# First layer's shift as two extra columns of keys, values and queries, and its scale weights loaded first

## The reference

```python
sh1, sc1, gt1, sh2, sc2, gt2 = modulation(cond, w_mod, b_mod)   # silu(cond) @ w_mod + b_mod
h = rms_norm(x, norm1_g) * (1.0 + sc1) + sh1
q, k, v, u = mixer_projections(h, w_in, ...)     # one product; q and k then normed per head
attn = block_attention(q, keys, vals)            # 8 heads, 2 key heads, head width 64
pooled = pool_mixer(u, w_pool, pool_scale)       # windowed mean minus self, 4 windows
x = x + gt1 * (concat(attn, pooled) @ w_out)
h2 = rms_norm(x, norm2_g) * (1.0 + sc2) + sh2
x = x + gt2 * conv_ffn(h2, w_up, conv_w, conv_b, w_down)
```

## Time and profile before

| | us |
|---|---|
| median of 3 runs (lowest, highest) | 1436.96 (1436.85, 1437.48) |
| the profiled execution | 1439.71 |
| its span, first to last instruction | 1437.9 |
| granted TensorE clock, mean | 0.996 |
| PE busy | 1405.4 (98%) |
| VectorE busy | 907.0 (63%) |
| ScalarE busy | 534.4 (37%) |
| GpSimd busy | 398.6 (28%) |

### The profile page before, as it was taken

One profiled execution on the slowest core, in us unless ns is written; L12 is line 12 of the kernel. 1 busy time (PEld: TensorE's weight loads), 2 busy tenths in 40 slices (PEclk: granted clock), 3 DMA queues, 4 the chain that ended last, 5 costly groups with the idle time before them and its releaser, 6 DMA issues.

```text
span 1437.9 us, 24974 instructions
## 1 busy us (share of the span) xinstructions
PE 1405.4 (98%) x9867; PEld 1347.5 (94%) x9867; DVE 907.0 (63%) x1429; ACT 534.4 (37%) x798; POOL 398.6 (28%) x273
## 2 busy tenths in 40 slices
PE   6999999999999999999999999999999999999998
PEld 3888889999999999999999877999999999999998
DVE  3548879897966478785775887369844323444333
ACT  5427863533231123332242687244232112332332
POOL 0165002053430033434214800213433101323321
PEclk9999999999999999999999999999999999999999
DMA  9752014253535334344413200224323312222321
GB/s 317 226 183 96 2 31 133 90 152 110 163 122 164 94 115 143 124 120 150 125 56 89 62 2 2 59 89 132 103 74 88 90 57 74 73 73 73 101 61 74
DMA packets 198158, 147.03 MB, mean 102 GB/s; under 512 B 4401, under 2 KB 187449, under 8 KB 197049
## 3 DMA queue, kind: packets, MB, share of 16 engines
q1 hardware_dynamic: 196592, 144.27, 32.8%
q10 hardware_dynamic: 1480, 1.57, 0.3%
HBM read 142.94 MB, written 2.88 MB: 101 GB/s over the span
## 4 chain that ended last, share of the span: by engine, by line
PE 83%; DVE 9%; ACT 2%; issue 2%; SPq 1%; DMA 1%; DVEq 0%; ACTq 0%
PE pair L1506 65%; PE pair L1522 7%; PE pair L1916 3%; PE pair L1961 3%; PE pair L1930 2%; DVE mod_acc L1073 2%; DVE conv L1423 1%; DVE in_lo L1139 1%; DVE w_lo L1050 1%; DVE norm_t L1129 1%; SPq L427 1%; DMA w_first<-in_w_mod_dram 1%; DVE small L1352 1%; PE pair L1759 1%; PE pair L1662 0%
## 5 line engine op out<-in xcount | busy, mean ns | idle before, releaser
L1506 PE MATMUL pair<-in_hi,w_hi 128*128 128x384 f32 x1728 | 395.7, 310 | 2.8 <-DVE w_lo L1050 2.8
L1506 PE MATMUL pair<-in_lo,w_hi 128*128 128x384 f32 x1728 | 394.6, 309 | 0.0
L1506 PE MATMUL pair<-in_hi,w_lo 128*128 128x384 f32 x1728 | 393.0, 308 | 0.0
L1423 DVE SCALAR_TENSOR_TENSOR conv<-pair,vec,conv 128x127 f32<-128x127 f32 x352 | 168.6, 542 | 192.8 <-ACT conv L956 192.4
L1506 PEld LDWEIGHTS pair<-in_hi,w_hi 128*128 128x128 f32 x1728 | 264.8, 188 | 8.3 <-DVE w_lo L1050 3.7
L1506 PEld LDWEIGHTS pair<-in_lo,w_hi 128*128 128x128 f32 x1728 | 265.3, 189 | 0.0
L1506 PEld LDWEIGHTS pair<-in_hi,w_lo 128*128 128x128 f32 x1728 | 264.0, 188 | 0.0
L653 POOL TENSOR_TENSOR silu_a<-silu_a,conv 128x640 f32<-128x640 f32 x44 | 108.6, 2469 | 538.7 <-DVE conv L1423 538.7
L956 ACT ACTIVATE conv<-pair,vec 128x640 f32<-128x640 f32 x88 | 77.8, 886 | 409.7 <-PE pair L1506 407.4
L1050 DVE TENSOR_TENSOR w_lo<-w_raw,w_hi 128x1024 fp32r<-128x1024 f32 (+1 forms) x148 | 195.6, 1322 | 38.3 <-ACT w_hi L675 38.0
L675 ACT ACTIVATE w_hi<-w_raw 128x1024 fp32r<-128x1024 f32 (+1 forms) x82 | 97.0, 1183 | 289.7 <-PE pair L1506 272.9
(11 more groups left out here) (210 smaller groups left out, 1773.1 us busy)
## 6 DMA issues: line engine op xcount, KB each, us to landing
w_raw<-in_w_up_dram SPq DMA_DIRECT2D x88, 512.0 KB, 3.8
mod_raw<-in_w_mod_dram SPq DMA_DIRECT2D x64, 512.0 KB, 4.2
w_raw<-in_w_down_dram SPq DMA_DIRECT2D x32, 704.0 KB, 4.6
w_raw<-in_w_in_dram SPq DMA_DIRECT2D x20, 512.0 KB, 4.1
w_first<-in_w_mod_dram SPq DMA_DIRECT2D x16, 512.0 KB, 9.3
w_raw<-in_w_out_dram SPq DMA_DIRECT2D x16, 512.0 KB, 4.0
mod_raw<-in_w_mod_dram SPq DMA_DIRECT2D x4, 1024.0 KB, 5.0
mod_acc<-in_w_mod_dram SPq DMA_DIRECT2D x4, 1024.0 KB, 5.0
```

The source lines that it names most:

```text
L1423: ins = dve.scalar_tensor_tensor(out=conv[:, s, d0:d1], in0=up_result(g, j, s)[:, d0 + sh:d1 + sh], scalar=v(L, V_TAP[t], s * NF + g * FG ...
L1506: ins = pe.matmul(dst[:, a:e], w[:, s, k, :], rhs[:, kk, a:e], start=first and r == 0, stop=last and r == 2)
```

## The change

The normalised features of layer 0 no longer contain the shift: `in_hi` and `in_lo` hold x times norm times gain, made in one operation for each segment. The shift itself becomes two columns (one for each conditioning) behind the 640 of each feature, split into high and low like the rest. Keys, values and queries of layer 0 are multiplied with 642 columns, and the product of the two last columns is added as a bias when ScalarE takes the tile out of PSUM, segment by segment. The pooled part u needs no shift, since a constant falls out of a mean minus self.

The modulation weights are loaded in eight parts of 1 MB: f = 0 to 3 scale, f = 4 to 7 shift. Only the scale parts stand before the first products. The sums of parts 4 and 5 stand ahead of tile 2, their turning behind it, those of parts 6 and 7 and `mod_second(0)` inside tile 3. Parts 6 and 7 are loaded into the place of the scaled x, after the last low part has been made. The rows of vectors are turned in two steps instead of one, the table for the root is loaded ahead of the squares, x tile 7 is copied by ScalarE instead of VectorE, and rows of the first modulation lie in `v_feat` instead of `mod_acc`. The diff, cut to its core:

```diff
+        XE_SCALAR, XE_VECTOR = [4, 6, 7], [0, 1, 2, 3, 5]
 
 
         with ExitStack() as inputs:
-            in_hi = sb("in_hi", [P, NK, T], F32R, at=inputs)
-            in_lo = sb("in_lo", [P, NK, T], F32R, at=inputs)
+            TX = T + 2
+            in_hi_x = sb("in_hi", [P, NK, TX], F32R, at=inputs)
+            in_lo_x = sb("in_lo", [P, NK, TX], F32R, at=inputs)
...
             def load_first(f):
 
-                if f >= N_FIRST:
-                    sp.wait_ge(s_mfirst, f - N_FIRST + 1)
-                for h in range(2):
-                    for ch in range(2):
-                        src = w_mod[0][h * D // 2:(h + 1) * D // 2, ch * D + f * 2 * P:ch * D + (f + 1) * 2 * P]
-                        sp.dma_start(w_first[:, f % N_FIRST, ch, h * NK // 2:(h + 1) * NK // 2, :],
-                                     src.rearrange("(i p) n -> p i n", p=P)).then_inc(s_first[2 * f + h], 16)
+                if f == 4:
+                    sp.wait_ge(s_mfirst, 1)
+                elif f == 5:
+                    sp.wait_ge(s_mfirst, 3)
+                elif f == 6:
+                    sp.wait_ge(s_h, 2 * NK)
+                ch, at = (1, f) if f < NK // 2 else (0, f - NK // 2)
+                src = w_mod[0][:, ch * D + at * 2 * P:ch * D + (at + 1) * 2 * P]
+                sp.dma_start(first_place[f], src.rearrange("(i p) n -> p i n", p=P)).then_inc(s_first[f], 16)
...
                 load_first(f)
-            for n in range(2, 4):
-                load_in(0, n)
+            load_in(0, 2)
+            load_first(4)
+            load_first(5)
+            load_in(0, 3)
+            load_first(6)
+            load_first(7)
             sp.dma_start(cst[:, P:n_const - P], consts[:, P:n_const - P]).then_inc(s_const, 16)
             load_second(0)
...
+            first_row(0)
+            x_copy(XE_SCALAR[0])
+            columns(0)
             hi(0, 0, NK)
-
-
+            x_copy(XE_SCALAR[1])
+            x_copy(XE_SCALAR[2])
+            hi(1, 1, NK)
...
-                        act_e.wait_ge(s_vec_t, L + 2)
-                        for t in range(3):
-                            ins = act_e.activation(vec[:, L, t, 0:N_ROWS[t]], pair[L][:, t * P:t * P + N_ROWS[t]], ACT.Copy)
-                        ins.then_inc(s_vec, 1)
-                    hi(1, 1, NK)
                 act_e.wait_ge(*((s_fmod, k + 1) if k < NK - 1 else (s_gain, 1)))
-                act_e.wait_ge(s_xhat, k + 1)
-                if k >= 2:
-                    act_e.wait_ge(s_h, 2 * (k - 1))
+                act_e.wait_ge(s_nt, 2 * (k + 1))
                 for ci, a, b in SEG:
-                    act_e.activation(sq[:, k % 2, a:b], xhat[:, k, a:b], ACT.Identity,
-                                     scale=gain[:, 0, 0, ci, k:k + 1],
-                                     bias=mod[:, 0, 0, ci, k:k + 1]).then_inc(s_nt, 1)
-                act_e.wait_ge(s_nt, 2 * (k + 1))
-                act_e.activation(in_hi[:, k, :], sq[:, k % 2, :], ACT.Copy).then_inc(s_hhi, 2)
+                    act_e.activation(in_hi[:, k, a:b], xhat[:, k, a:b], ACT.Copy,
+                                     scale=gain[:, 0, 0, ci, k:k + 1]).then_inc(s_hhi, 1)
+                if k in (2, 4):
+                    first_row(k // 2 + 1)
+                if k == 6:
+                    columns(1)
...
                     e = e_of(n)
+                    shifted = L == 0 and n >= IN_K
+                    if shifted:
+                        columns_ = pair[n % 2][:, LIN0 + T:LIN0 + TX]
+                        act_e.activation(shift_out[:, n - IN_K, 0, :], columns_, ACT.Copy).then_inc(s_shift_out, 1)
+                        if n >= IN_Q:
+                            act_e.activation(shift_out[:, n - IN_K, 1, :], columns_, ACT.Copy,
+                                             scale=v(L, V_QG, 0)).then_inc(s_shift_out, 1)
+                        act_e.wait_ge(s_shift_out, n - IN_K + 1 + max(0, n - IN_Q + 1))
+
+                    def evict(dst, func, own=0):
+                        for ci, a, b in SEG:
+                            ins = act_e.activation(dst[:, a:b], lin[n % 2][:, a:b], func,
+                                                   bias=shift_out[:, n - IN_K, own, ci:ci + 1],
+                                                   scale=v(L, V_QG, 0) if own else 1.0)
+                        return ins
...
-            for k in range(2):
-                scaled_x(k)
-            lo(0, 0, NK)
+                for t in range(2):
+                    if f < NK // 2:
+                        m = 2 * f + t
+                        dve.tensor_scalar(gain[:, 0, 0, :, m], first_sum[:, f % 2, t, :], v(0, V_N1, m),
+                                          first_gain[:, m:m + 1], ALU.mult, ALU.add)\
+                           .then_inc(*((s_fmod, 1) if m < NK - 1 else (s_gain, 1)))
+                    else:
+                        m = 2 * f + t - NK
+                        ins = dve.tensor_scalar(mod[:, 0, 0, :, m], first_sum[:, f % 2, t, :], v(0, V_BMOD, m), None, ALU.add)
+                        if m == NK - 1:
+                            ins.then_inc(s_mod, 2)
...
+                dve.wait_ge(s_shift_hi, 1)
+                dve.tensor_tensor(in_lo_x[:, :, T:TX], mod[:, 0, 0, :, :].rearrange("p c k -> p k c"),
+                                  in_hi_x[:, :, T:TX].bitcast(F32), ALU.subtract).then_inc(s_shift, 1)
+
             dve.wait_ge(s_vec, 1)
             dve.scalar_tensor_tensor(out=first_gain[:, :], in0=v(0, V_BMOD, NK, NK), scalar=1.0, in1=v(0, V_N1, 0, NK),
                                      op0=ALU.add, op1=ALU.mult).then_inc(s_fgain, 1)
             dve.wait_ge(s_fgain, 1)
             first_mod(0)
+            dve.wait_ge(s_bc, 1)
+            scaled_x(0)
             lo(1, 1, NK)
+            scaled_x(1)
             for k in range(NK):
+                for ci, a, b in SEG:
+                    dve.wait_ge(s_hhi, 2 * k + 1 + ci)
+                    dve.scalar_tensor_tensor(out=in_lo[:, k, a:b], in0=xhat[:, k, a:b], scalar=gain[:, 0, 0, ci, k:k + 1],
+                                             in1=in_hi[:, k, a:b].bitcast(F32), op0=ALU.mult,
+                                             op1=ALU.subtract).then_inc(s_h, 1)
+                if k % 2 == 0 and k // 2 + 1 < NK // 2:
+                    first_mod(k // 2 + 1)
                 if k + 2 < NK:
                     scaled_x(k + 2)
-                if k % 2 == 1 and k + 1 < NK:
-                    first_mod((k + 1) // 2)
-                dve.wait_ge(s_hhi, 2 * (k + 1))
...
+                    if L == 0 and n == 2:
+                        first_mod(4)
+                        first_mod(5)
                     if n >= IN_Q:
                         shuffle(e_of(n))
                     if n == N_IN - 1:
@@ -1331,6 +1402,10 @@
                         shuffle(0)
                     if 2 <= n < 2 + NPOOL:
                         window_end(n - 2)
+                    if L == 0 and n == 2:
+                        first_mod(6)
+                        first_mod(7)
+                        shift_low()
...
+            def first_sums(f):
+                pe.wait_ge(s_first[f], 16)
+                if f == 1:
+                    pe.wait_ge(s_vec, 1)
+                elif f == 4:
+                    pe.wait_ge(s_nt, 2 * NK)
+                elif f == 6:
+                    pe.wait_ge(s_u, 6)
+                if f >= 2:
                     pe.wait_ge(s_fsum, f - 1)
-                for i in range(4):
-                    ins = pe.matmul(first_bank(f)[i * QUAD:(i + 1) * QUAD, :].rearrange("p (c n) -> p c n", c=2),
-                                    cond_cols[:, 4 * h + i, :], w_first[:, f % N_FIRST, :, 4 * h + i, :],
-                                    start=h == 0, stop=h == 1)
-                if h == 1:
-                    ins.then_inc(s_mfirst, 1)
+                for k in range(NK):
...
+                if k == 3:
+                    first_sums(0)
+                if k == 4:
+                    rows_turned(0)
+                if k == 5:
+                    first_columns(0)
             pe.wait_ge(s_rstd, 1)
             spread_tiles(range(NT)).then_inc(s_bc, 1)
-            for h in range(2):
-                first_sums(0, h)
-            N_ROW_DMAS = 5 + 4 + 3 + DEPTH
-            pe.wait_ge(s_rows, 16 * N_ROW_DMAS)
-            for L in range(DEPTH):
-                x_emptied(NK - 2 + L)
-                for t in range(3):
-                    ins = pe.transpose(pair[L][:, t * P:t * P + N_ROWS[t]], rows[0:N_ROWS[t], L, t, :],
...
-
-                    def first_ahead(k):
-                        f = k // 2 + 1 if k % 2 == 0 else k // 2 + 2
-                        if k == 0:
-                            first_sums(1, 0)
-                        if f < NK // 2:
-                            first_sums(f, 1 if k % 2 == 0 else 0)
+                    x_emptied(NK - 2)
+                    x_emptied(NK - 1)
+                    keep_busy(3, pair[0][:, 0:P])
 
```

(63 more changed lines are left out.)

108 lines of the change are left out of this document (57 added, 51 removed).

## The result

| | us |
|---|---|
| kernel before, median of 5 runs | 1437.29 |
| changed kernel, median of 5 runs (lowest, highest) | 1443.70 (1443.4, 1444.8) |
| ratio, 95% interval | 1.0047 (1.0033 to 1.0062) |
| profiled execution of the changed kernel | 1444.8, span 1443.0 |
| forecast | 1434.8 (1431.0 to 1439.0) |

What follows compares the result with a forecast made beforehand. PE was taken as the bound, with the start bound by bytes in the SP queue. Front gain 5.0 - 1.9 - 0.9 - 0.1 = 2.1, say 2.2 us, off the median 1436.96 gives 1434.8, range 1431.0 to 1439.0.

Steps and rivals of the forecast that it cites:

- Point 9: Behind the first scores: later stages are untouched and PE-bound, so what is gained at the first scores stays gained.
- Point 8: Tiles 4 to 9: the two extra columns cost 0.1 us in the sum, bounds 0 and 2.2.
- Points 1 to 3: Front: f1 lands at 21.9, first product at 24.4 (gain 7.0), third tile ends at 52.5 (gain 8.9).
- rival B: New front: the clock falls again (2.5 us) or f1 is late (1.5), giving 1436.5 to 1437.5; chance 0.20.
- point 2: From f1 to first product: PE starts at 24.4 against 31.46; table load hidden, even at the quoted 2.66 us.
- Point 5: Tile 3, SP's new wait: w_in 4 lands at 60.3, s_shift at 65.4, tile 4 starts at 65.5; front gains 5.0.
- rival C: Queue behind SP's new wait: w_in 4 after 60.5 loses time one for one; 1441.0 at 250 GB/s; chance 0.08.
- Point 6: Evictions of tiles 4 to 9: ScalarE needs 1.0 to 1.1 more a query tile; PE waits 1.9 in tile 9.
- Point 7: Tile 9 to first scores: serial ScalarE adds 1.05, VectorE wins part back; 0.9 lost, bounds 0.3 and 1.1.

Runs made afterwards that it cites:

- b_pitch642: Kernel before with only the rows of in_hi and in_lo widened to 642 floats (2568 bytes), cond_rows moved to make room: 1441.74 us, ratio 1.0033.
- a_turn672: a_pitch672 plus constants and mod_second 0 and 1 issued ahead of f6 and f7, and ScalarE's copy second_rows ahead of k_out: 1431.03 us, ratio 0.9954.
- a_pitch656: Changed kernel with rows of in_hi and in_lo of 656 floats (2624 bytes) in place of 642: 1444.01 us.
- a_pitch672: Changed kernel with rows of in_hi and in_lo of 672 floats (2688 bytes), shift_out and first_gain moved to make room: 1436.38 us, ratio 0.9993.
- a_plain_evict: Changed kernel with the evictions of the kernel before for tiles 4 to 9 (no shift_out, no bias, one segment each): 1439.98 us.
- a_loads: Changed kernel with the constants and mod_second 0 and 1 issued ahead of loads f6 and f7: 1440.30 us, ratio 1.0023 of before.
- b_base64: Kernel before with an unused 64-byte array ahead of in_hi, moving array starts, pitch still 2560 bytes: 1435.48 us, ratio 0.9991.
- b_base32: Kernel before with an unused 32-byte array ahead of in_hi, starts at multiples of 128 bytes, pitch 2560: 1427.08 us, ratio 0.9950, in two groups.
- b_mix: Kernel before with only in_lo moved, to 32 bytes beyond a multiple of 64, in_hi at a multiple of 64, pitch 2560: 1443.09 us, ratio 1.0037.
- b_off48: Kernel before with in_hi and in_lo both starting 48 bytes beyond a multiple of 64, pitch 2560: 1447.12 us, ratio 1.0068.

## Why the prediction was wrong

The waits of the front and of tile 9 were read rightly. The time was lost by the price of a matmul, which the sum put at almost nothing, by a baseline that the median run doesn't have, and by VectorE's small and late instructions beside GpSimd.

- **Point 9, later stages untouched, failed.** "What is gained at the first scores stays gained" is true for waiting, not for the price of a matmul. The changed kernel loses 3.3 us behind the first scores. *b_pitch642*, where nothing but the rows changed, loses 5.5 there and 4.8 in its median.
- **Point 8 named the cause and mis-sized it.** It says that no row shows a row of `in_hi` that starts 8 bytes off, and bounds the cost at 2.2, for the six tiles with the extra columns. But the pitch belongs to the array, and every product that reads it in both layers pays: 5184 matmuls, not 144. It measured 4.3 behind the first scores, where I had taken 0.1. The extra columns themselves were sized well: with the pitch mended a tile with them takes 7.26, and one of the same shape without them (at 203.15 in *a_turn672*) 7.22, 0.2 us in all.
- **The sum's own baseline failed.** The gain was read off an execution with half clock from 29 to 35, 2.75 us over the median, and taken from the median in full. I had written how the two stand to each other, and then carried 5.0 over as if the median run had that stretch too. With tile 4 at 67.6 in executions without it, the gain at 65.5 would have been 2.1, and the forecast 2.1 - 1.9 - 0.9 - 0.1 = -0.8, that is 1437.8: no gain at all, or next to none if the median run has a short fall. What the front gave is less still: tile 4 starts at 67.25 to 67.64 in the four profiles with this front (the changed kernel, *a_pitch656*, *a_pitch672*, *a_plain_evict*), 0.5 ahead of 67.8 at most.
- **Points 1 to 3 held**: f1 22.2 (21.9), first product 24.67 (24.4), third tile's end 52.1 (52.5), no half clock there (rival B). The table load took 1.28 (9.08 to 10.36) and the next activation began at 10.38, less than the figure that point 2 quotes.
- **Point 5 held up to VectorE.** w_in 4 was in at 60.8 (60.3); the columns of f6 became possible at 62.21 (62.2), and PE waited 0.9 for them. Then two `first_mod` took 2.0 more than sized, beside two instructions of GpSimd: `s_shift` at 67.4, not 65.4. I had taken their price from rows without GpSimd at work. The fall of the clock in tile 4 (1.6) comes and goes with the execution: of the four profiles with this front and this wait, the changed kernel and *a_pitch672* have it, *a_pitch656* and *a_plain_evict* don't. *a_loads*, without the wait, is 3.0 to 3.4 faster in the median. That is rival C's mechanism, the queue behind SP's new wait, at much less than its price, and coming on top rather than in place.
- **Point 6 held**: PE's wait in the middle of tile 9 is 1.66 (1.9), and it goes with the additions (*a_plain_evict*) or with an earlier copy (*a_turn672*).
- **Point 7 was short.** From the end of tile 9 to the first scores it took 7.5 before and 9.3 after, 1.7 more (0.9, bounds 0.3 and 1.1). ScalarE's root comes 0.9 later behind tile 9 (1.05 worked out), but PE's transposes, which wait for it, only 0.5, since PE had other work in between before. The other 1.2 is VectorE's. It was to win here and lost, since its `w_lo` (2.30) now comes just behind the start of an instruction of GpSimd and ends 1.5 behind PE's transposes (the line of GpSimd first):

```profile
127.63 1.28 POOL L649 TENSOR_TENSOR rope<-rope,cst 128x512 f32<-128x512 f32 x1
...
127.69 2.30 DVE L1105 TENSOR_TENSOR w_lo<-w_raw,w_hi 128x1024 fp32r<-128x1024 f32 x1
...
132.01 0.39 PE L2016 MATMUL pair<-k_hi,q_st 128*128 128x256 f32 x1 [0.49 <-DVE in_lo L1377]
```

In the kernel before the same split starts 0.2 ahead of GpSimd's instruction, takes 1.21, and is done when the transposes are:

```profile
126.20 1.21 DVE L1050 TENSOR_TENSOR w_lo<-w_raw,w_hi 128x1024 fp32r<-128x1024 f32 x1
...
129.70 0.39 PE L1916 MATMUL pair<-k_hi,q_st 128*128 128x256 f32 x1 [0.30 <-DVE in_lo L1309]
```

The ledger, without half clock on either side: first mark at 123.7 to 124.1 before (*b_base64*, *b_pitch642*) and 126.4 with the changed front (*a_pitch656*), so 2.3 to 2.7 lost; 0.8 from the mark to the first scores, by VectorE; 3.3 behind them, by the rows; together 6.4 to 6.8, and 6.4 was measured.

The edit's idea was sound in front and tail. With rows of 2688 bytes, two loads in another order and one copy earlier (*a_turn672*) it is 6.2 us under the kernel before. Of these, 3.1 lie between the marks (1223.4 - 1220.3), and I put them down to the layout. The kernel before was not run with rows of 2688, so it might have these 3.1 without the edit; the edit's own part is the other 3.1, most of it ahead of the first mark (121.5 against 123.7 to 124.1; tile 4 at 64.4 against 67.5 to 67.8).

## What to carry to other kernels

An edit that widens an array changes the address of every row in it: count every product that reads the array, not only those that use the new columns, and compare one long untouched piece of PE work (here 480 matmuls) before and after. When the profiled execution is slower than the median, find the stretch that makes it so before an edit is credited with removing it. For VectorE instructions on the path, tiny ones too, take the price they have beside GpSimd (an instruction of GpSimd longer), and when a wait is put into a queue, move behind it only what has to be there.

## What the runs showed of the hardware

- TensorE's rate on 32-bit operands depends on where the rows of the moving operand lie in SBUF: 68.9 to 71.5 us for the same 480 matmuls at the same granted clock (1.00), *b_base32* and *b_mix*; 70.46 with rows of 2560 bytes and 71.13 with rows of 2568 in the otherwise same program.
- With array starts at multiples of 128 bytes one program (*b_base32*) ran in two groups of times, 1425.3 to 1427.1 and 1435.2 to 1438.1, at a mean clock of 0.999 in each.
- A two-element VectorE instruction took 0.22 to 0.23 us alone and 1.34 and 1.13 beside instructions of 1.29 us on GpSimd; a subtraction of 1024 columns took 1.21 when it started 0.2 ahead of GpSimd's instruction, and 1.22 (*a_pitch672*) or 2.30 (the changed kernel) where the two starts were less than 0.1 apart; where it took 1.22, GpSimd's took 2.38 in place of 1.28.
- The granted clock fell to 0.50 behind a gap of 3.46 us in PE's work in the kernel before; behind a gap of 1.97 it stayed at 1.00 in *b_base64* and fell in *b_off48*.
